# Low parts of the hidden tiles at the border to the down projection: GpSimd in place of VectorE

## What is computed

```python
def _swiglu(h, w_gate, w_up, w_down):
    return (jax.nn.silu(h @ w_gate) * (h @ w_up)) @ w_down

f1 = _swiglu(h, w['w_ffn_gate'][l, 0], w['w_ffn_up'][l, 0], w['w_ffn_down'][l, 0])
x = x + (0.5 * (1.0 + mod[:, 2]) * f1).astype(x.dtype)
```

## Time and profile before

| What | us |
|---|---|
| Median of 3 runs (2858.98 to 2865.41) | 2860.62 |
| The profiled execution | 2879.42 |
| Its span, first to last instruction | 2877.7 |
| PE busy | 2642.8 |
| DVE busy | 1719.4 |
| ACT busy | 1047.2 |
| POOL busy | 775.2 |

### The profile page before, as it was taken

The page is one execution under the profiler, slowest core; times in us unless marked ns, Lnnn a source line. Parts: engine busy times, 40 slices in busy tenths (PEclk is TensorE's granted clock), DMA queues, the critical chain, the costliest instruction groups (busy, mean ns, idle before and its releaser), DMA issues. The chain is left out here.

```text
span 2877.7 us, 52261 instructions
## 1 busy us (share of the span) xinstructions
PE 2642.8 (92%) x22580; PEld 2461.4 (86%) x22580; DVE 1719.4 (60%) x2353; ACT 1047.2 (36%) x1484; POOL 775.2 (27%) x530
## 2 busy tenths in 40 slices
PE   3999999999689998899999899999999498899998
PEld 0999988899378876899998899998889378799998
DVE  2868725743466645788852687852632356877824
ACT  2444414322533322444432434442421433444523
POOL 2665201000011021365510156610000121456301
PEclk7999999999689988999999999999999589999999
DMA  6222455721100013332245432255651113322324
GB/s 247 74 89 96 145 182 163 250 85 46 57 2 3 3 55 128 118 103 96 95 169 172 130 103 96 92 173 169 217 187 52 50 20 132 109 92 94 100 81 127
DMA packets 82349, 316.74 MB, mean 110 GB/s; under 512 B 9400, under 2 KB 14408, under 8 KB 80584
## 3 DMA queue, kind: packets, MB, share of 16 engines
q1 hardware_dynamic: 82120, 313.40, 32.7%
HBM read 302.63 MB, written 10.74 MB: 109 GB/s over the span
## 5 line engine op out<-in xcount | busy, mean ns | idle before, releaser
L165 DVE TENSOR_TENSOR weights_r<-work,weights_r 128x1024 fp32r<-128x1024 f32 (+2 forms) x318 | 436.5, 1373 | 356.8 <-ACT weights_r L161 356.5
L161 ACT ACTIVATE weights_r<-work 128x1024 fp32r<-128x1024 f32 (+2 forms) x318 | 313.1, 985 | 584.5 <-PE banks L860 341.8
L756 POOL TENSOR_TENSOR rows<-rows,consts 128x288 f32<-128x288 f32 (+3 forms) x64 | 88.4, 1381 | 691.5 <-ACT consts L967 691.5
L858 PE MATMUL banks<-low_r,weights_r 128*128 128x288 f32 (+2 forms) x1112 | 270.1, 299 | 0.0
L856 PE MATMUL banks<-h_r,weights_r 128*128 128x288 f32 (+1 forms) x904 | 226.0, 305 | 42.0 <-DVE big_r L419 25.8
L858 PE MATMUL banks<-big_r,weights_r 128*128 128x288 f32 (+2 forms) x960 | 244.1, 299 | 0.0
L856 PE MATMUL banks<-low_r,weights_r 128*128 128x288 f32 (+2 forms) x832 | 215.5, 306 | 27.1 <-DVE weights_r L165 18.3
L773 PE MATMUL banks<-h_r,weights_r 128*128 128x288 f32 x788 | 233.1, 296 | 1.6 <-DVE weights_r L165 0.8
L774 PE MATMUL banks<-big_r,weights_r 128*128 128x288 f32 x788 | 232.3, 295 | 0.0
L775 PE MATMUL banks<-h_r,weights_r 128*128 128x288 f32 x788 | 232.1, 295 | 0.0
L860 PE MATMUL banks<-h_r,weights_r 128*128 128x288 f32 (+1 forms) x904 | 221.5, 300 | 0.0
(11 more groups left out here) (550 smaller groups left out, 7079.1 us busy)
## 6 DMA issues: line engine op xcount, KB each, us to landing
work<-w_ff_dram SPq DMA_DIRECT2D x130, 512.0 KB, 3.7
h<-w_mod_dram SPq DMA_DIRECT2D x48, 768.0 KB, 5.3
work<-w_down_dram SPq DMA_DIRECT2D x66, 512.0 KB, 3.5
consts<-w_ff_dram SPq DMA_DIRECT2D x64, 512.0 KB, 3.6
work<-w_mod_dram SPq DMA_DIRECT2D x32, 768.0 KB, 9.1
work<-w_in_even_dram SPq DMA_DIRECT2D x24, 512.0 KB, 3.7
big_buf<-w_mod_dram SPq DMA_DIRECT2D x16, 768.0 KB, 6.0
consts<-w_down_dram SPq DMA_DIRECT2D x22, 512.0 KB, 3.6
```

Of the source, the lines that this page charges most:

```text
L161: return act.activation(high, raw, ACT.Copy)
L165: return engine.tensor_tensor(low, raw, high.bitcast(F32), ALU.subtract)
L756: pool.tensor_tensor(k.rows[:, c], k.rows[:, c], k.square[:, c], ALU.add).then_inc(added, 1)
L858: pe.matmul(out[a], high[:, w], x[a][1], start=False, stop=False)
```

## The change

The fifteen `hidden_low` instructions of each of the four up stages leave VectorE's program. The same instructions, with the same waits and the same operands, stand in GpSimd's program, behind the weight sums of the last unit of the stage and ahead of the memset of the down stage, in the order of the tiles: 0, 8, 9, ..., 21. ScalarE's part, the semaphores and TensorE's waits stay as they are.

```diff
--- before.py
+++ after.py
@@ -740,6 +740,10 @@
                             if n:
                                 pool.wait_ge(low_done, sevens[n - 1].pieces[3][0] + 1)
                             pool.tensor_tensor(mixed_4, a12, s2, ALU.subtract).then_inc(weights_mixed, 1)
+                        for kt in LATE:
+                            at = hidden(kt)
+                            pool.wait_ge(late_high, late_count(stage, kt))
+                            split_low(pool, k.big_buf[:, at], k.low_r[:, at], k.big_r[:, at]).then_inc(late_low, 1)
                     if stage in mod_in:
 
                         pool.wait_ge(piece_done, stage.first + 1)
@@ -1102,11 +1106,6 @@
                     dve.wait_ge(tokens_high, mix.split_count(name))
                     split_low(dve, mix.mixed[name], mix.high[name], mix.low[name]).then_inc(tokens_low, 1)
 
-                def hidden_low(up, kt):
-                    at = hidden(kt)
-                    dve.wait_ge(late_high, late_count(up, kt))
-                    split_low(dve, k.big_buf[:, at], k.low_r[:, at], k.big_r[:, at]).then_inc(late_low, 1)
-
                 def add(u):
 
                     e = u.stage.edges
@@ -1229,9 +1228,6 @@
                         low_act(u)
                     if i in tokens_at:
                         mixed_low(*tokens_at[i])
-                    if i in late_at:
-                        for kt in late_at[i][1]:
-                            hidden_low(late_at[i][0], kt)
                     for stage in stages:
                         if stage.kind == "proj_even" and i == stage.first:
                             for b in range(STAGES):
```

## The result

| | before | after |
|---|---|---|
| Median of 6 runs each, side by side | 2863.82 us | 2885.11 us |
| Ratio, 95% interval | | 1.0056 (1.0033 to 1.0079) |
| Span of the profiled execution | 2877.7 | 2880.6 |
| TensorE from tile 7's last product to the end of the first down unit, four borders | 21.0, 20.2, 20.4, 20.3: 81.9 | 23.9, 23.2, 23.9, 23.9: 94.9 |

The change makes the kernel slower by 0.56%, 16 us (9 to 23). This ratio is not the quotient of the two medians, which is 1.0074 (21 us) and lies inside the interval too. Put on the 2860.62 us of the forecast, the ratio gives 2876.6 us.

A forecast was written before the change was run, and what follows sets the result against it. TensorE was taken as the bound, busy 2642.8 of 2877.7 us. Border losses of +2.1, +2.4, +2.4 and +2.3 us made +9.2, so 2860.62 + 9.2 gave 2870 us, range 2859 to 2880.

The forecast's parts named there:

- the two engines exclude each other on reads: GpSimd and VectorE instructions with two SBUF operands wait for each other: sum +9.2 us with it, -2 without.
- the third sum: L1085, weights of the third piece on VectorE, second border: starts at 1460.7 instead of 1462.52, 1.9 us won.
- the tail: Last tiles, 19 to 21, on GpSimd at a border: at the second, tile 21 starts 2.1 us later.
- the forecast's own spread: +4 to +15 us, from who gets the path first, up to one instruction (1.3 us) a border.
- The walk: Second border step by step, the two engines taking turns: tile 7's low ends at 1466.66, tile 21 starts 2.1 us later.
- the sum over the borders: Four borders, +2.1 at the second and +2.4, +2.4 and +2.3 at the others: +9.2 us in all.
- That the shared path isn't the limit: Rival: GpSimd's and VectorE's reads don't meet, or VectorE goes first; -6.4 and +4.2, together -2 us; chance 0.10.
- That GpSimd is cheap, like L2317: Rival: a low takes 1.17 us on GpSimd, less in a queue; +2 us; chance 0.13.
- That GpSimd is dear, for the rounded type: Rival: a low takes 1.76 us on GpSimd, by the rounded type or like L281; +30 us; chance 0.07.
- All sixty were moved: Answers the rival that the change doesn't do what it says: 0 us; chance 0.02.
- GpSimd's memset: L110, behind tile 21: some 13 us later, costs nothing since its reader is sixteen pieces later.
- 7.1 us all that the change can win: TensorE's waits at the four borders: 6.4 us for tile 7's low, 0.7 us for tile 19's.

The follow-up runs named there:

- the memsets: Kernel before plus 44 GpSimd memsets of 352 columns at each border, writing only, in place of extra subtractions: ratio 0.9987, borders -0.8 us.
- the second trace: The changed kernel run once more with no edit: ratio 1.0059 against the kernel before, borders 92.2 us, +10.3.
- the extra reads: Kernel before plus 22 GpSimd subtractions of 352 columns at each border, both operands in SBUF, results unused: ratio 1.0117, borders +36.4 us.
- the order with earlier highs: Kernel before, all lows on VectorE, 10 to 12 behind tile 7's, highs and lows of 19 to 21 one step earlier: ratio 0.9967, borders -8.7 us.
- the kernel with the earlier highs: Changed kernel with ScalarE's highs of tiles 19 to 21 one step earlier: ratio 1.0044 against the kernel before, borders 93.0 us, +11.1.

## Why the prediction was right

**Right.** Slower was forecast at 0.68, by the mechanism that the runs then showed: the two engines exclude each other on reads (+36 us for reads that nobody waits for, none for writes), the third sum comes earlier but the gain is lost on the way to tile 7, and the tail is late. The Trainium skill, SBUF — State Buffer, section "Who interferes with whom", names the write-only instruction as free of the exclusion; the trace agrees with 747 to 759 ns for VectorE's lows beside the memsets. The result, 1.0056, lies within the range once put on the same base (2876.6 us in 2859 to 2880). It is +16 us there, just above the forecast's own spread of +4 to +15, and the quotient of the medians, 1.0074, would give 2881.8 us, above the range. So the direction and the mechanism are firm, and that the size lies within is in part luck.

**The walk, step by step.** The trace after can be laid over the walk for the second border by adding 2.47 us (1459.09 less 1456.62, the last products of the up stages). Then the weights of piece 2 end at 1461.3 (the walk said 1460.7), the third sum starts at 1461.2 (1460.7), the weights of piece 3 end at 1463.4 (1462.8), the gate-up product at 1465.3 (1464.75), tile 7's low at 1467.2 (1466.66), tile 21's at 1481.5 (1480.7). Each step up to tile 7 has the right length to 0.1 us; the walk is 0.5 to 0.6 us early from its first step on, and 0.8 at tile 21. TensorE waited 0.9 us longer for tile 7 and not 0.3.

**The term that was mis-sized** is the sum over the borders: +9.2 us, where the two traces of the changed kernel have 13.0 and 10.3. Three things are in it.

First, TensorE's clock, which the walk took to be 2.4 GHz throughout, as it is in all four stretches of the trace of before. In the first trace after it falls to 1.2 GHz behind the wait for tile 7 at the first, third and fourth border, each time for some 3.4 us, and comes back. The second piece (tiles 8 to 15) ends 1.5 us later for it, 16.3 us behind the last product of the up stage in place of 14.8 at the fourth border, and by the way shown above (late highs, GpSimd's gap of 1.66 or 1.67 us ahead of tile 19) the last border takes 23.9 us and not the 22.7 of the second trace, which has the clock at full speed at all borders. The third takes 23.9 and 22.9. These two, 2.2 us together, are most of the 2.7 us between the traces. At the first border the fall adds nothing to the difference (23.9 in both), since in the second trace the first low started 1.2 us later against TensorE.

Second, the offset between TensorE and the two splitting engines, which the walk took from one trace. At the second border ScalarE's high of tile 0 came 5.42 us ahead of the last product before, 4.84 after, and 5.43 in the second trace after. All that follows on the shared path is later by these 0.6 us: tile 7's low ended 8.11 us behind the last product where the walk has 7.57, and with the walk's offset, in the second trace, it ended at 7.57. The border took 23.25 us and 22.72.

Third, a low that follows another on GpSimd without VectorE between them took 1.42 us less the 0.04 by which the two overlap, 1.38 and not about 1.3. The last low of the second trace ends 21.89 us behind the last product, where the walk has 21.6.

With the clock at full speed, in the second trace, the four borders took 23.87, 22.72, 22.93 and 22.70 us, and the walk had 23.4, 22.35, 22.8 and 22.6 (the four of before plus 2.4, 2.1, 2.4 and 2.3). The fifteen lows took 26.50, 26.55, 26.50 and 26.53 us there from the first start to the last end, where the walk has 26.3. The first border is the longest since its first low started only 3.46 us ahead of the up stage's last product, and the others' 4.66, 4.39 and 4.66. For that border the prediction shows no walk. The one of the second border, begun 3.56 us ahead as in the trace of before, comes to 23.5 us; the 0.4 us to 23.87 are 0.2 of longer lows, 0.1 of the start and 0.1 behind the last low.

**The two halves.** The walk put 0.3 us of loss ahead of tile 7 and 1.8 behind it, at the second border. Made one at a time, they cost 0.36 and 2.1 us there, 2.2 and 9.6 us over all four, each with one fall of the clock in it.

**The rivals.** That the shared path isn't the limit (-2 us) fell with the extra reads and with the lows ahead of tile 7 alone. That GpSimd is cheap, like L2317, fell with 1.41 us at best for a low; the prediction took L2317 to have one repeated operand, but its code repeats both (`to_broadcast` on each), so it was further from a low than it was taken for. That GpSimd is dear, for the rounded type, fell with the same number, since L718 takes 1.40 for plain float32. All sixty were moved: the page counts 60 instructions less on DVE and 60 more on POOL.

**What was costed at nothing.** GpSimd's memset is 14 us later at the second border (1478.99 plus the 2.47 of the overlay, against 1467.50 before; the prediction said some 13), and no engine waits longer for it. The prediction called 7.1 us all that the change can win; the order with earlier highs took 8.7 us off the borders. The step that it didn't take was to ask what else could free the third sum: it named the three lows ahead of it, and moving just these behind tile 7 is worth 7.1 us at the borders, more than the 6.4 us of waits for tile 7 that it had counted.

## What to carry to other kernels

Before work goes from VectorE to GpSimd, count the instructions with two SBUF operands that both engines have to get through in the stretch, at the price of the engine that runs each: on reads they are one queue, and here it was full (26 us of work for 24 us of room). An idle engine in the page's first part is no spare capacity if it comes in by the same door. And where a wait is caused by what stands ahead of an instruction, try the order first: three instructions a border moved behind another took 7.1 us off the four borders of a trace, where fifteen a border moved to another engine added 10 to 13. The runs show that gain clear of no change only together with the earlier highs (0.9967).

## What the runs showed of the hardware that was not expected

TensorE's clock can fall on a short wait. Before, its waits for tile 7 were 2.1, 1.4, 1.5 and 1.4 us, and it kept 2.4 GHz behind all of them. In the changed kernel they were 1.7, 2.3, 1.8 and 1.7 us, and it fell to 1.2 GHz behind the 1.7, 1.8 and 1.7 but not behind the 2.3; in the second run of the same kernel (1.5, 1.7, 2.0 and 1.7 us) it fell behind none. With only the lows ahead of tile 7 on GpSimd it fell at the wait of 2.2 us and not at those of 1.5, 1.7 and 1.7; with only those behind, at 2.2 and not at 1.4, 1.5 and 1.4; with the earlier highs, behind 1.7 and 1.8 and not behind 1.5 and 2.1. So of fifteen waits for tile 7 of 1.7 to 2.3 us seven cost the clock, and their length doesn't tell which. In the waits of 5.9 to 7.0 us of the kernel with the extra reads it fell all four times. The fall cost up to 1.2 us at a border of the changed kernel, and some 1.4 at the third border with only the lows ahead on GpSimd.

Behind none of the waits for tile 7 of 1.5 us or less did it fall. But a shorter wait isn't safe by that: at the fourth border of the kernel with the earlier highs the clock was at full speed behind the wait of 2.1 us for tile 7, and fell some 13 us later, behind waits of 0.2, 1.3 and 0.3 us for tiles 18, 19 and 20. A stretch of that trace there, columns as above:

```profile
2744.50:2747.50 3.00, 2.68 (x13) 2.25 (x12) 0.00 (x0) 0.00 (x0) 1.93 (x2) 0.66 0.26 108
```

The exclusion is exact to some 0.02 us and independent of the tile: in the changed kernel VectorE's 1024-wide low ended 1.08 us after GpSimd's, its 768-wide 0.82 and its 576-wide 0.61, and GpSimd's low 1.26 to 1.30 us after VectorE's instruction. When both have work queued they take turns one by one; in no case did VectorE wait for two of GpSimd's lows in a row (no instruction of 576 columns took over 1.98 us at a border). A memset on GpSimd, 393 ns for 352 columns, passes beside VectorE's reads unhindered (392 to 402 ns, all 176). And the rounded result type costs GpSimd nothing that can be seen: 1.41 us at best against 1.40 for float32.
